# Hyena taps and turning moved inside a weight block, sums of taps moved two slots ahead, in a two-layer hybrid encoder

## The reference: what is computed

```python
h = (h @ w3.astype(f32) + b3.astype(f32)).reshape(L, 2, n_ch)
h = h * jnp.exp(-t[:, :, None] * jnp.abs(deltas))
h_full = jnp.concatenate([h[:, 0], jnp.zeros((1, n_ch), f32), h[1:, 1][::-1]], axis=0)
h_full = h_full / jnp.sum(jnp.abs(h_full), axis=0, keepdims=True)
return jnp.fft.rfft(h_full, axis=0).reshape(L + 1, HY_ORDER, W_B)
...
for n, gate in enumerate((x1, x2)):
    z_f = jnp.fft.rfft(z, n=2 * L, axis=1)
    conv = jnp.fft.irfft(z_f * filt_f[:, n], n=2 * L, axis=1)[:, :L]
    z = gate * (conv + bias[n].astype(f32) * z)
```

```python
lifted = jnp.einsum('blnc,ncd->blnd', branches, w_lift[i])
gates = jax.nn.sigmoid(gate_logits.reshape(bsz, L, N_BRANCH, D_MODEL))
mixed = jnp.sum(gates * lifted, axis=2) @ w_out[i]
```

## Time and profile before

| | us |
|---|---|
| median of three runs | 2689.77 |
| lowest, highest run | 2687.35, 2689.95 |
| the profiled execution's own time | 2684.76 |
| its span in the trace | 2683.2 |
| PE busy | 2596.8 (97%) |
| VectorE busy | 1862.0 (69%) |
| ScalarE busy | 1288.6 (48%) |

### The profile page before, as it was taken

One profiled execution on the slowest core, in us unless ns is written; L12 is line 12 of the kernel. 1 busy time (PEld: TensorE's weight loads), 2 busy tenths in 40 slices (PEclk: granted clock), 3 DMA queues, 4 the chain that ended last, 5 costly groups with the idle time before them and its releaser, 6 DMA issues.

```text
span 2683.2 us, 41615 instructions
## 1 busy us (share of the span) xinstructions
PE 2596.8 (97%) x13736; PEld 2157.6 (80%) x13736; DVE 1862.0 (69%) x3251; ACT 1288.6 (48%) x2334; POOL 111.6 (4%) x206
## 2 busy tenths in 40 slices
PE   7999999999999999999989999999999999999998
PEld 6889999976776768898778999898877767688986
DVE  7788778735776767556678878876367757765666
ACT  5555555543444334443465555556344433344535
POOL 2100000000000000000021000000000000000000
PEclk9999999999999999999999999999999999999998
DMA  7544444434443324555564444443344533355554
GB/s 250 164 147 152 152 145 148 157 114 150 150 163 124 128 96 163 187 175 172 165 205 154 152 146 151 148 151 131 138 145 151 173 102 126 102 187 187 173 172 144
DMA packets 115956, 411.83 MB, mean 153 GB/s; under 512 B 15460, under 2 KB 15514, under 8 KB 115584
## 3 DMA queue, kind: packets, MB, share of 16 engines
q1 hardware_dynamic: 107424, 391.17, 43.8%
q0 software_dynamic: 8416, 19.18, 2.2%
HBM read 403.99 MB, written 6.29 MB: 153 GB/s over the span
## 4 chain that ended last, share of the span: by engine, by line
PE 91%; DVE 4%; issue 2%; ACT 2%; DMA 1%; PEldq 0%; PEld 0%; DVEq 0%; POOL 0%; POOLq 0%; ACTq 0%
PE bank L1620 29%; PE bank L1660 19%; PE bank L1662 10%; PE bank L2000 6%; PE bank L1577 5%; PE bank L1595 4%; PE bank L1750 2%; PE bank L1732 2%; PE bank L1713 2%; PE bank L1920 2%; PE bank L1934 1%; PE bank L1818 1%; PE bank L1698 1%; PE bank L1900 1%; PE bank L1842 1%
## 5 line engine op out<-in xcount | busy, mean ns | idle before, releaser
L381 ACT ACTIVATE WH<-ring 128x512 fp32r<-128x512 f32 x1364 | 854.8, 631 | 1176.4 <-PE bank L1620 515.3
L395 DVE TENSOR_TENSOR WL<-ring,WH 128x512 fp32r<-128x512 f32 x852 | 573.3, 688 | 456.2 <-ACT WH L381 454.1
L1660 PE MATMUL bank<-XX,WH 128*128 128x512 f32 x2304 | 820.9, 400 | 27.7 <-DVE XX L564 15.4
L1662 PE MATMUL bank<-XX,WL 128*128 128x256 f32 x2304 | 644.5, 280 | 0.0
L1660 PEld LDWEIGHTS bank<-XX,WH 128*128 128x128 f32 x2304 | 435.7, 189 | 128.5 <-DVE XX L564 15.4
L1620 PE MATMUL bank<-WH,XX 128*128 128x512 f32 x1536 | 493.0, 402 | 4.4 <-issue 3.5
L386 DVE TENSOR_TENSOR WL<-ring,WH 128x512 fp32r<-128x512 f32 x512 | 350.5, 687 | 138.1 <-ACT WH L381 134.0
L1662 PEld LDWEIGHTS bank<-XX,WL 128*128 128x128 f32 x2304 | 437.4, 190 | 0.0
L1620 PEld LDWEIGHTS bank<-WH,XX 128*128 128x128 f32 x1536 | 290.1, 191 | 83.1 <-issue 22.4
L1620 PE MATMUL bank<-WL,XX 128*128 128x512 f32 x768 | 303.6, 395 | 0.0
L1620 PEld LDWEIGHTS bank<-WL,XX 128*128 128x128 f32 x768 | 146.6, 191 | 31.8
(11 more groups left out here) (311 smaller groups left out, 3340.3 us busy)
## 6 DMA issues: line engine op xcount, KB each, us to landing
ring<-in_blocks SPq DMA_DIRECT2D x738, 512.0 KB, 3.3
ARENA<-in_bc POOLq DMA_DIRECT2D x2, 2048.0 KB, 8.6
ARENA<-in_decay POOLq DMA_DIRECT2D x8, 512.0 KB, 4.0
ARENA<-in_x SPq DMA_DIRECT2D x4, 512.0 KB, 8.4
u_scratch<-ARENA POOLq DMA_DIRECT2D x16, 128.0 KB, 2.5
ARENA<-u_scratch POOLq DMA_DIRECT2D x64, 32.0 KB, 3.2
y_scratch<-ARENA POOLq DMA_DIRECT2D x16, 128.0 KB, 2.0
ARENA<-y_scratch POOLq DMA_DIRECT2D x64, 32.0 KB, 2.7
```

What stands on the lines that cost most here:

```text
L381: nc.scalar.activation(wh[q], raw(which[0], q), ACT.Copy).then_inc(wh_ready[q], 1)
L395: vec.tensor_tensor(wl[q], raw(which[0], q), wh[q].bitcast(F32), ALU.subtract).then_inc(w_used[slot(which[0], half)], 1)
L1660: ins = mm(bank[b][:, :], h, xx[:, :, k, :], start=(k == 0), stop=(k == DT - 1), skip_group_check=True)
L1662: ins = mm(bank[b][:, 0:T], l, xh[:, k, :], start=False, stop=(k == DT - 1), skip_group_check=True)
```

## The change

Three steps move on PE, and one on VectorE with them:

- the taps of chunk 1 (slot 3) stand between the second and the third quarter of that slot's weight block, instead of ahead of the block;
- the turning (slot 6) stands between the second and the third quarter of its block, instead of ahead;
- the sums of taps stand ahead of the block of slot 6 instead of in slot 8, and fill bank 4 instead of bank 6. The reciprocal on VectorE moves to slot 6 as well, behind the first half of the next block's low part.

token_block gets a parameter between, a function that is called ahead of the third quarter. The table of fills and the function hyc follow: in a layer bank 4 has two fills more, bank 6 two fewer.

```diff
-    "hyc":  [4, 4, 4, 4, 18, 18, 20, 18],
+    "hyc":  [4, 4, 4, 4, 20, 18, 18, 18],
...
-        def hyc(o, step, n=0, b=4):
+        def hyc(o, step, n, b):
 
-            at = {"taps": 2 * n, "dft": 2 * n + 1, "turn": 4, "fwd": 5 + n, "inv": 7 + n, "sums": 6}[step]
-            return o * 10 + at + (step == "inv" or step == "fwd" and n == 1) if b == 6 else o * 9 + at
+            at = {"taps": 2 * n, "dft": 2 * n + 1, "sums": 4, "turn": 4, "fwd": 5 + n, "inv": 7 + n}[step]
+            return o * 10 + at + (step in ("turn", "fwd", "inv")) if b == 4 else o * 9 + at
...
+                    if s_ == 6:
+                        full(4, "hyc", hyc(o, "sums", 0, 4))
+                        free(v.reciprocal(NS[:, o * 8:o * 8 + 8], bank[4][:, 0:8]), 4)
                     if s_ in (7, 8, 9):
-                        if s_ == 8:
-                            full(6, "hyc", hyc(o, "sums", 0, 6))
-                            free(v.reciprocal(NS[:, o * 8:o * 8 + 8], bank[6][:, 0:8]), 6)
                         product(o, (0, 1, 1)[s_ - 7], (0, 0, 1)[s_ - 7])
...
-                def token_block(b, x, j, n, *which):
+                def token_block(b, x, j, n, between, *which):
 
                     for q in range(4):
+                        if q == 2 and between is not None:
+                            between()
                         part_made(q, *which)
...
                 def tap_sums(o):
                     pe.wait_ge(sums_ready, layer * CHUNKS + (o * 2 + 2))
-                    take_bank(6, "hyc", hyc(o, "sums", 0, 6))
+                    take_bank(4, "hyc", hyc(o, "sums", 0, 4))
...
-                    if s_ in (0, 3):
-                        taps(o, s_ // 3)
+                    between = None
+                    if s_ == 0:
+                        taps(o, 0)
+                    if s_ == 3:
+                        between = lambda: taps(o, 1)
                     if s_ in (2, 5):
                         filter_dft(o, s_ // 3)
                     if s_ == 6:
-                        turn_z(o)
+                        tap_sums(o)
+                        between = lambda: turn_z(o)
                     if s_ == 7:
                         forward(o, 0, 0)
                         forward(o, 0, 1)
                     if s_ in (8, 9):
                         forward(o, 1, s_ - 8)
-                    if s_ == 8:
-                        tap_sums(o)
                     if s_ in (10, 11):
                         inverse(o, s_ - 10)
```

More of the change, by code:

```diff
@@ L468, in _ @@
                     if c:
-                        pool.wait_ge(psum_free[7], read_out(layer, "hyc", 7, hyc((c - 1) // 2, "taps", (c - 1) % 2)))
+                        pool.wait_ge(psum_free[7], read_out(layer, "hyc", 7, hyc((c - 1) // 2, "taps", (c - 1) % 2, 7)))
                     else:
@@ L480, in _ @@
                     elif c == 2:
-                        pool.wait_ge(psum_free[7], read_out(layer, "hyc", 7, hyc(0, "inv", 1)))
+                        pool.wait_ge(psum_free[7], read_out(layer, "hyc", 7, hyc(0, "inv", 1, 7)))
                     pool.sem_inc(dec_free, 1)
@@ L983, in even_odd @@
                 def even_odd(o, c):
-                    out_of(7, "hyc", hyc(o, "taps", c))
+                    out_of(7, "hyc", hyc(o, "taps", c, 7))
                     dve.wait_ge(taps_ready, layer * CHUNKS + (o * 2 + c + 1))
                     if c:
-                        full(7, "hyc", hyc(o, "dft", 0))
+                        full(7, "hyc", hyc(o, "dft", 0, 7))
                     f, b = HH[:, 0:2 * CW], HH[:, 2 * CW:4 * CW]
@@ L1637, in token_block, with gated_block @@
                             ins[1].then_inc(parts_used[q], 1)
-                def gated_block(stage, g, p, x, y, *which):
+                def gated_block(stage, g, p, x, y, *which, between=None):
                     b = 0 if p < 4 else 2
@@ L1644, in gated_block @@
                             take_bank(b + t, stage, g)
-                    token_block(b, y if b else x, p - 4 if b else p, 2 if b else 4, *which)
+                    token_block(b, y if b else x, p - 4 if b else p, 2 if b else 4, between, *which)
                 def wide_half(b, half, *which):
@@ L1886, in tap_sums @@
                     pe.wait_ge(sums_ready, layer * CHUNKS + (o * 2 + 2))
-                    take_bank(6, "hyc", hyc(o, "sums", 0, 6))
+                    take_bank(4, "hyc", hyc(o, "sums", 0, 4))
                     for j in range(8):
-                        ins = mm(bank[6][:, j:j + 1], SUM[:, j * P:(j + 1) * P], ones[:, 0:1], start=True, stop=True)
+                        ins = mm(bank[4][:, j:j + 1], SUM[:, j * P:(j + 1) * P], ones[:, 0:1], start=True, stop=True)
                         if j < 7:
                             release(ins)
-                    done(ins, 6)
+                    done(ins, 4)
                 def filter_dft(o, c):
@@ L1959, in _ @@
                         pe.wait_ge(yl_ready, layer * 4 + 2)
-                    gated_block("hyc", k // 6, k % 6, (xh, xl), yc, B_LIFT + 24 + k)
+                    gated_block("hyc", k // 6, k % 6, (xh, xl), yc, B_LIFT + 24 + k, between=between)
                 yb = (split(YBH, WT), split(YBL, WT))
```

## The result

The changed kernel takes 2670.66 us, the median of four runs (2666.46 to 2671.09), against 2689.86 for the kernel before in the same comparison (2687.35 to 2693.46): a ratio of 0.9927, with a 95% interval of 0.9914 to 0.9941, or 15.9 to 23.1 us won. The forecast was 2672.3. The profiled execution took 2666.46 us (forecast 2667), its span is 2664.9 us, 18.3 shorter than before.

A forecast was written before the change was run, and what follows sets the result against it. PE, busy for 97% of the span, was taken to bound the kernel. The terms -12.7 + 9.5 + 6.0 - 20.3 = -17.5 us bring 2689.77 us to 2672.3 us; range 2660 to 2682 us.

The forecast's parts named there:

- The taps: Slot three, chunk 1: inside the block the taps take 3.73 us without waiting, instead of 6.47 or 8.17; -12.7 us.
- The wait at the turning: Slot six: PE stands still 3.8 us a pass until VectorE's reciprocal frees bank 4; before, 2.5 us in two pieces.
- The transposes: Slot six: the turning's 16 transposes take 2.36 us a pass, within the 13.7 us to block six's end.
- The clock behind the wait: Slot six: the lower clock follows the turning's wait in all four passes, 1.5 us each; +6.0 us, bounds nothing and 11.
- Wait and transposes: Slot six without the lower clock: four stretches of 13.7 us against 45.2 us before in sum; +9.5 us.
- Both slot-six terms: Slot six: the longer stretch with wait and transposes, +9.5 us, and the lower clock behind the wait, +6.0 us.
- Slots seven to nine: Forward transform to block nine, without the sums: 30.7 us a pass, with 0.8 us of PE wait in block nine; -20.3 us.
- Register instructions: Added semaphore bookkeeping, 57 instructions a layer on PE, 43 on VectorE, 17 on ScalarE: taken to cost 0.
- Rival 2: Chunk 1 taps keep single file inside the block, 5.61 us instead of 3.73; 7.5 us lost, 2680 us; chance 0.09.
- rival 5: Added register instructions come due on PE, some 184 at 0.05 us, 9 us; 2681 us; chance 0.08.
- Rival 3: The wait at the turning is short, about 1.5 us, perhaps without lower clock; 15 us, 2657 us; chance 0.10.
- Rival 4: Lower clock stays through block six's rest and the forward transform, 9.6 us a pass; slower, 2705 us; chance 0.05.

The follow-up runs named there:

- the early reciprocal: The changed kernel with the reciprocal of the sums moved on VectorE ahead of the unfolding of slot five; 2646.71 us, ratio 0.9842 to the kernel before.
- the shared count: The changed kernel with bank 5 counting as many fills a layer as bank 4, so their semaphore targets share a register; 2669.51 us, ratio 0.9932.

## Why the prediction was right, step by step

**The taps.** Forecast -12.7 us, measured -12.5. The reason held too: with the banks free as the matmuls issue, 3.75 us and no wait, in the change and with the taps alone. Only the picture of before was too simple: not all matmuls went in single file, two of the four banks were still filled side by side (the last section shows it).

**The wait at the turning.** Forecast 3.8 us a pass, for the reciprocal; measured 3.7, by that line, four times. Walking both engines' orders up to the point where they meet gave the wait to 0.1 us, and moving the reciprocal took it away.

**The transposes.** This term was mis-sized. I took 2.36 us, the busy time of the old stretch less that of a clean block; at full clock and without pauses the 16 transposes take 1.83 us, as the run with the early reciprocal shows. The old stretch had had PE running them in pieces. Over four passes that is 2.1 us too dear.

**The clock behind the wait.** Forecast 1.5 us in each pass, 6.0. Transposes and the second half of block six take 6.30, 6.34, 5.91 and 6.31 us (14.68, 14.72, 14.28 and 14.68 less what lies ahead), clean they take 1.83 + 2.82 = 4.65: 1.65, 1.69, 1.26 and 1.66, in all 6.3. The sum was right, the place was not: I had it in the second half of block six, it begins anywhere from some 0.6 us ahead of the first transpose (third pass) to some 1.2 us behind it (second pass), and ends in that half (0.90 in the first pass). The working also gave 1.9 us as the longest wait ahead of the sums; it was 1.3 in each pass. That the sum came so near is in part luck: with the same wait the shared count shows one pass without it and two at 2.5 us, 6.5 in all. On the rule of the Trainium skill weighed there ("TensorE: Matmul & The Clock Gate", section "Why this matters for your kernels"), that PE should not idle between bursts: the trace of after agrees, with four of four at 3.7 us of idle, and it was right against the count of two in four that I set beside it. With the shared count it was three of four at the same 3.7 us, so the rule held in most passes and not in each. Three of four at 2.5 us, and two of four with the sums alone and 0.3 us, that rule of the Trainium skill doesn't foretell.

Wait and transposes were forecast at +9.5, and are +6.9 (13.2 less the clock's 6.3). Both slot-six terms together: forecast +15.5, measured +13.2.

**Slots seven to nine.** Forecast -20.3 us, measured -19.8, at a granted clock of 1.00. VectorE's part of the working held; PE's wait in block nine is 0.4 us and not 0.8, since block eight now stands directly behind a transform and lasts 5.89 us, as block nine did before (889.75 to 895.64), and not the 5.68 of a block behind transposes that I used: PE comes to the place later, VectorE at the time that was worked out.

**Register instructions.** Forecast 0; no difference with 222 instructions fewer, and the span lost all but 0.8 us of what the three stages won.

**The rivals.** Rival 2 and rival 5 were tested and fell. Rival 3 (a short wait) failed in this kernel, and its price can now be read: without any wait some 22 us more; I put 15, since I let the wait keep 1.5 us a pass, 6 in all. Rival 4 (the lower clock stays into the forward transform, slower) fell: that stretch is at 1.00 in all passes.

So the prediction was right through terms that each held within 2.6 us; the sum of -17.5 became -19.1 in the stages, mainly for the transposes (2.1 us).

**What stays open.** When the lower clock follows. The same wait of 1.3 us with the same one-column matmuls had it in four passes of four before and in two of four with the turning alone; the turning ahead of its block, with 2.5 us of wait in two pieces, had it in two of four before and in four of four with the taps alone; inside the block it came in three of four after 2.5 us and in eleven of twelve after 3.7 us. No run here settles what decides it.

## What to carry to other kernels

When a step is moved into a place where it shares a buffer with another, follow the buffer's release on the engine that gives it: here 0.2 us of work, queued behind 4.5 us of other work, took back more than half of what the change could win (21.8 of 41.0 us), and moving three lines gave it back. Price idle time of a matmul engine with what follows it at a lower clock, pass by pass, and don't add gains of edits that fill the same gap. A step that only waits for its buffers loses that wait inside a block of independent matmuls, if the block's first part is as long as the wait.

## What the runs showed of the hardware

The clock can fall in a wait or behind it: in the first pass of after PE idles from 848.4 us with the granted clock at 1.00 up to 852.4, and all but the first transposes run at half of it; in the third it is at 0.50 before PE starts again. With the sums alone it fell in two passes with no wait over 0.3 us ahead of it. Transposes stretch with the clock as matmuls do, 1.83 us at full clock against 3.16 at a mean of 0.56.

Two streams of matmuls that use rows 0 to 63 and rows 64 to 127 of the array run beside each other if both have their bank: 3.75 us against 6.47 for the same eight matmuls, with a busy time of 5.61 in the slow case: of the 2.7 us lost only 0.9 are the wait. The slow case of before in pieces, bank 4 alone, then banks 6 and 5 together behind the wait, then bank 7 alone:

```profile
821.43:823.41 1.98, 1.98 (x5) 0.67 (x4) 1.45 (x3) 0.63 (x1) 0.00 (x0) 1.00 0.66 246
824.27:826.10 1.83, 1.83 (x9) 0.90 (x10) 1.23 (x2) 0.00 (x0) 0.00 (x0) 1.00 0.68 264
826.10:827.90 1.80, 1.80 (x6) 0.56 (x3) 0.00 (x0) 0.00 (x0) 0.00 (x0) 1.00 0.00 0
```

One bank alone takes as long as two side by side, so the same matmuls took three rounds, where chunk 0 takes two (3.73 us).

Kernels that hardly differ there had the lower clock behind the same gap in four and in two of their passes (behind the sums), or in four and in three (at the turning). A gain read from one such stretch carries an uncertainty of 1.5 to 2.5 us a pass, and single parts measured to a few us can owe that much to it.
